# Value and gate groups of four attention blocks as pairs with two Strassen blocks each, and the attention tail moved into the next pair

## The reference, cut to what matters

```
proj = h @ w_in                      # (256 x 2048) @ (2048 x 14336), columns xr yr q k v g_rnn g_attn
q = partial_rope(q); k = partial_rope(k)
p = softmax(causal(q @ k.T * 128 ** -0.5))      # 16 heads of 128, 256 x 256 each
o = p @ v
attn_out = o @ w_attn_proj
merged = sigmoid(g_rnn) * rnn_out + sigmoid(g_attn) * attn_out
x = x + merged @ w_mix_out
```

## Time and profile before

| | us |
|---|---|
| median of 3 runs (1747.55 to 1747.8) | 1747.65 |
| the profiled execution | 1748.19 |
| its span in the trace | 1745.9 |
| PE busy | 1734.6 (99%) |
| VectorE busy | 1327.0 (76%) |
| ScalarE busy | 986.8 (57%) |
| granted TensorE clock | 0.999 |

### The profile page before, as it was taken

How to read it: one execution, slowest core, us unless ns; L and a number is a source line. 1 busy time by engine, 2 the same in 40 slices (tenths; PEclk the granted TensorE clock), 3 DMA queues, 4 the chain that set the end, 5 groups by cost and what they waited for, 6 DMA issues and landing times.

```text
span 1745.9 us, 20385 instructions
## 1 busy us (share of the span) xinstructions
PE 1734.6 (99%) x7905; PEld 1439.8 (82%) x7905; DVE 1327.0 (76%) x1457; ACT 986.8 (57%) x1228; POOL 28.8 (2%) x54
## 2 busy tenths in 40 slices
PE   9999999999999999999999999999999999999998
PEld 7888888888888888888888888888888888888886
DVE  7577687887575757678765579888888888888887
ACT  6767678554555555555465465555555545555554
POOL 1100000000000000000000000000000000000000
PEclk9999999999999999999999999999999999999999
DMA  9565655666565655556865455566566566566663
GB/s 339 174 203 163 212 184 163 201 211 195 158 215 168 217 169 185 174 166 217 271 186 188 140 174 184 191 196 195 196 197 219 187 211 198 183 193 196 214 194 119
DMA packets 176048, 338.23 MB, mean 194 GB/s; under 512 B 10704, under 2 KB 15312, under 8 KB 175696
## 3 DMA queue, kind: packets, MB, share of 16 engines
q1 hardware_dynamic: 173376, 327.98, 59.4%
q0 software_dynamic: 1296, 5.24, 1.0%
q10 hardware_dynamic: 1280, 3.71, 0.5%
HBM read 334.80 MB, written 2.10 MB: 193 GB/s over the span
## 4 chain that ended last, share of the span: by engine, by line
PE 98%; DVE 1%; ACT 0%; DMA 0%; issue 0%; ACTq 0%; POOLq 0%; POOL 0%; DVEq 0%
PE group L486 29%; PE group L488 28%; PE group L487 28%; PE side L486 3%; PE side L487 3%; PE side L488 3%; PE side L549 2%; PE side L683 0%; PE side L667 0%; DMA x_T_in<-in_x_T 0%; PE side L621 0%; PE side L620 0%; PE side L619 0%; DVE x_res L1603 0%; PE side L665 0%
## 5 line engine op out<-in xcount | busy, mean ns | idle before, releaser
L858 ACT ACTIVATE w_hi<-w_raw 128x1024 fp32r<-128x1024 f32 x612 | 618.9, 1024 | 489.7 <-PE group L488 475.7
L1253 DVE TENSOR_TENSOR w_lo<-w_raw,w_hi 128x1024 fp32r<-128x1024 f32 x612 | 707.9, 1179 | 236.7 <-ACT w_hi L858 231.1
L486 PE MATMUL group<-w_hi,x_hi 128*128 128x512 f32 x1460 | 573.3, 393 | 0.6 <-DVE w_lo L1321 0.6
L488 PE MATMUL group<-w_hi,x_lo 128*128 128x512 f32 x1460 | 568.8, 390 | 0.0
L487 PE MATMUL group<-w_lo,x_hi 128*128 128x512 f32 x1460 | 568.2, 389 | 0.0
L486 PEld LDWEIGHTS group<-w_hi,x_hi 128*128 128x128 f32 x1460 | 274.2, 188 | 58.6 <-DVE w_lo L1253 2.3
L488 PEld LDWEIGHTS group<-w_hi,x_lo 128*128 128x128 f32 x1460 | 274.0, 188 | 57.7
L487 PEld LDWEIGHTS group<-w_lo,x_hi 128*128 128x128 f32 x1460 | 274.3, 188 | 55.5
L858 ACT ACTIVATE w_hi<-w_sums 128x1024 fp32r<-128x1024 f32 x98 | 103.9, 1061 | 179.3 <-PE group L488 150.3
L1253 DVE TENSOR_TENSOR w_lo<-w_sums,w_hi 128x1024 fp32r<-128x1024 f32 x98 | 119.9, 1224 | 92.1 <-ACT w_hi L858 92.1
L486 PE MATMUL group<-w_hi,inner_hi 128*128 128x512 f32 x274 | 107.0, 391 | 0.2 <-DVE x_res L1603 0.2
(11 more groups left out here) (329 smaller groups left out, 1792.8 us busy)
## 6 DMA issues: line engine op xcount, KB each, us to landing
w_raw<-in_w_in SPq DMA_DIRECT2D x223, 512.0 KB, 4.2
w_raw<-in_w_ffn_gate SPq DMA_DIRECT2D x88, 512.0 KB, 3.9
w_raw<-in_w_ffn_up SPq DMA_DIRECT2D x88, 512.0 KB, 4.5
w_raw<-in_w_ffn_down SPq DMA_DIRECT2D x88, 512.0 KB, 5.0
w_raw<-in_w_rnn_proj SPq DMA_DIRECT2D x32, 512.0 KB, 4.9
w_raw<-in_w_attn_proj SPq DMA_DIRECT2D x32, 512.0 KB, 4.6
w_raw<-in_w_mix_out SPq DMA_DIRECT2D x32, 512.0 KB, 4.9
w_raw<-in_w_xkv SPq DMA_DIRECT2D x16, 512.0 KB, 3.8
```

Of the source, the lines that this page charges most:

```text
L486: nc.tensor.matmul(out, h, whi[:, s, k, :], start=start, stop=False)
L488: return nc.tensor.matmul(out, l, whi[:, s, k, :], start=False, stop=stop)
L858: nc.scalar.activation(whi[:, s, ks], src[:, ks], ACT.Copy).then_inc(hi_ready[s], 1)
L1253: V_.tensor_tensor(wlo[:, s, ks], src[:, ks], whi[:, s, ks].bitcast(F32), ALU.subtract).then_inc(w_ready[s], 1)
```

## The change

The groups v and g_attn of each attention block become one pair with the plan "O0 O1 O2 W3 O4 W5 O6 O7", so 20 chunks (steps 0 to 19) in place of 16, with A of the two Strassen blocks at steps 6 and 12. KEY_PLAN becomes the same plan. They share the input sums x_sums. v is folded in v_tok, the gate in its columns of sig_attn (`fold_of` now takes the half). In the new pair both transposes stand at step 2, the scores, the mask and the maxima at step 4, and the exponentials at steps 6 and 7. What followed them (division, transposes of the probabilities, product with v, v_hi and v_lo) moves, as `attention_end`, into the next pair: division at step 1, transposes at step 3, product with v at step 5, v_lo at step 6; ScalarE also scales v at step 0 and makes the gate's tanh at step 1 there. PE gets a wait for the mask ahead of chunk A, and the wait for v_lo ahead of the first chunk D of that next pair stays.

```diff
-KEY_PLAN = "O0 O1 W3 O2 O4 W5 O6 O7".split()
+KEY_PLAN = "O0 O1 O2 W3 O4 W5 O6 O7".split()
+VALUE_PLAN = "O0 O1 O2 W3 O4 W5 O6 O7".split()
...
# PE
+            def attention_end(c, j):
+
+                if c == 3:
+                    pe.wait_ge(sem("folded"), folds)
+                    pe.wait_ge(sem("prob"), j + 1)
...
+                    last.then_inc(sem("prob_T_ps"), 1)
+                if c == 5:
+                    pe.wait_ge(sem("prob_T"), j + 1)
+                    pe.wait_ge(sem("v_scaled"), j + 1)
...
+                        attention_end(c, j - 1)
                         if kind == "A" and kp == FIRST_SUM[first]:
-                            pe.wait_ge(sem("sums_lo"), 2)
                             pe.wait_ge(sem("folded"), folds)
                         if kind == "D" and kp == FIRST_SUM[first]:
                             pe.wait_ge(sem("attn_lo"), j)
                     folds += 1
-                for c in gemm_of("v", j, xhi, xlo):
+                first = ("v", j)
+                for c, kind, kp in pair_of(first, xhi, xlo, ks_hi, xs_lo, K_SUMS):
                     if c == 2:
                         pe.wait_ge(sem("k_rot"), j + 1)
+                        if folds > KG // 2:
+                            pe.wait_ge(sem("folded"), folds)
                         transpose(ktok, side[0], "k_T_ps")
-                    if c == 3:
                         pe.wait_ge(sem("q_rot"), j + 1)
                         transpose(qtok, side[1], "q_T_ps")
-                    if c == 5:
+                    if c == 4:
...
+                    if kind == "A" and kp == FIRST_SUM[first]:
+                        pe.wait_ge(sem("sums_lo"), 2)
+                        pe.wait_ge(sem("masked"), j + 1)
+                folds += 1
...
# ScalarE
+                first = ("v", j)
+                for c in splits(N0[first], len(STEPS[first])):
+                    first_fold(first, c)
...
-                for c in splits(N0["g_attn", j], CG):
-                    if c in (0, 1):
+                    if c in (6, 7):
                         act.wait_ge(sem("neg_max"), j + 1)
-                        for b in range(2 * c, 2 * c + 2):
+                        for b in range(2 * (c - 6), 2 * (c - 6) + 2):
...
# VectorE
+            def attention_end(c, j):
+
+                if c == 1:
+                    dve.wait_ge(sem("prob_exp"), j + 1)
+                    then(V_.reciprocal(rsum[:, :, :], psum_[:, :, :]))
...
+                if c == 6:
+                    dve.wait_ge(sem("attn_hi"), j + 1)
...
```

More of the change, by code:

```diff
@@ L103 @@
     elif _stage == "q" and _j > 0:
+        continue
+    elif _stage == "v":
+        PLACED.append(((_stage, _j), ("g_attn", _j), VALUE_PLAN))
+    elif _stage == "g_attn":
         continue
@@ L302, in slot_of, with fold_of @@
             return n % R, n // R
-        def fold_of(first):
-            return {"k": kq_fold, "attn_out": attn_fold}.get(first[0], fold)
+        def fold_of(first, half):
+            if first[0] == "v":
+                return sig_attn[:, :, first[1] * GW:(first[1] + 1) * GW] if half else vtok[:, :, :]
+            return {"k": kq_fold, "attn_out": attn_fold}.get(first[0], fold)[:, half]
         def raw_of(n):
@@ L381, in _ @@
                     pair(("k", j), (w_in,) * 2, 0, [IN_COLS[name] + j * GW for name in ("k", "q")])
-                in_group("v", j)
-                in_group("g_attn", j)
+                pair(("v", j), (w_in,) * 2, 0, [IN_COLS[name] + j * GW for name in ("v", "g_attn")])
             for q in range(0, KG, 2):
@@ L1066, in _ @@
                         first_fold(first, c)
-                        if c == 5 and j in (1, 2):
+                        attention_end(c, j - 1)
+                        if c == 12 and j in (1, 2):
                             mem_squares(2 * (j - 1))
@@ L1089, in _ @@
                                                             bias=nmax[:, tt, b:b + 1], accum_out=psum_[:, tt, b:b + 1])
-                        if c == 1:
+                        if c == 7:
                             last.then_inc(sem("prob_exp"), 1)
[L1092 to L1102, removed]
-                        evac_in("g_attn", j, [sig_attn[:, tt, j * GW:(j + 1) * GW] for tt in range(TT)], hrstd["x"], ACT.Tanh)
             def merge_hi(j):
@@ L1402, in fold_rest @@
             def fold_rest(first, c):
-                at_, fold = last_sum(first), fold_of(first)
+                at_, fold = last_sum(first), [fold_of(first, half) for half in range(2)]
                 if at_ is not None and c == at_ + 1:
@@ L1408, in fold_rest @@
                     wait_product(dve, N0[first] + c)
[L1409 to L1413 removed]
+                    then(V_.tensor_tensor(fold[1][:, 0, :], fold[0][:, 0, :], P6, ALU.subtract))
+                    then(V_.tensor_tensor(fold[0][:, 1, :], fold[1][:, 0, :], P7, ALU.subtract))
+                if at_ is not None and c == min(at_ + 2, len(STEPS[first]) - 2):
+                    V_.tensor_tensor(fold[1][:, 1, :], Q5, fold[0][:, 1, :], ALU.subtract)
+                    then(V_.tensor_tensor(fold[1][:, 0, :], Q5, fold[1][:, 0, :], ALU.subtract))
                     dve.sem_inc(sem("folded"), 1)
@@ L1418, in join @@
                 p, _ = buf_of(GI[first] + half)
-                fold = fold_of(first)
+                fold = fold_of(first, half)
                 wait_product(dve, end)
                 if last_sum(first) is None:
-                    V_.tensor_copy(fold[:, half], gps[p][:, :, :]).then_inc(taken[p], 1)
+                    V_.tensor_copy(fold, gps[p][:, :, :]).then_inc(taken[p], 1)
                 else:
-                    V_.tensor_tensor(fold[:, half], fold[:, half], gps[p][:, :, :], ALU.add).then_inc(taken[p], 1)
+                    V_.tensor_tensor(fold, fold, gps[p][:, :, :], ALU.add).then_inc(taken[p], 1)
             V_.memset(xTp[:, :, :], 0.0).then_inc(sem("pad_zero"), 1)
@@ L1553, in _ @@
                             join(first, half, END[("k", "q")[half], j])
-                for c in splits(N0["v", j], CG):
+                first = ("v", j)
+                count = len(STEPS[first])
+                for c in splits(N0[first], count):
+                    fold_rest(first, c)
                     if c == 0 and j > 0:
```

102 lines of the change are left out of this document (53 added, 49 removed).

## The result

| | median of its runs, us | runs (lowest to highest) | ratio to before [95%] |
|---|---|---|---|
| before | 1747.72 | 6 (1747.55 to 1747.97) | |
| changed | 1756.03 | 6 (1755.05 to 1756.41) | 1.0046 [1.0036, 1.0056] |

The account below looks back on a forecast made before the run. PE, busy 99% of the span, was taken to bound the kernel. New waits of 13.3 us less 5.4 us for 24 matmuls saved gave 7.9 us slower, 1755.5 us; 8-in-10 range 1750 to 1759.

Parts of the forecast that it names:

- 1: exponentials, 4 times, with the table load: Exponentials behind each block's first Strassen block make w_lo late: 1.85 us in each of 4 blocks, plus 1.4 once.
- 2: transposes of q, 4 times: Both transposes at step 2: PE waits for the rotation of q, 0.5 us a block with the restart.
- 3: v_lo ahead of D, 4 times: v_lo on VectorE behind w_lo of the next pair's first D comes late: 0.5 us a block.
- 4: division of the last block: In the first attn_out pair the division ends after PE wants it: 0.5 us once, with the restart.
- Place 1: Exponentials behind the first Strassen block: O4a 0.55 us late, second block's A 1.7 late; 1.85 a block with the restart.
- the restart: PE's cost of starting again after a wait: 0.17 us on top of each wait.
- (a): Rival: the gain lands and PE never waits, 1742.2 us; chance 0.07.
- (b): Rival: the exponentials cost nothing, the other waits leave 4.5 us against 5.4 saved, 1746.8 us; chance 0.07.
- (c): Rival: half the exponentials' cost, the sums being done before the late w_lo, 1752 us; chance 0.08.
- (d): Rival: waits drop PE's clock to 1.2 for a Strassen block each, 19 us more, 1775; 0.06 with other waits past 1759.
- (e): Rival: the change doesn't do what it says; given no chance.
- The table load: In block 0, between w_hi and the first exponential on ScalarE: 1.4 us once; by the skill's figure 1.3 us larger.

Follow-up runs that it names:

- experiment 1: The changed kernel with the two halves of the exponentials at steps 8 and 9 in place of 6 and 7: 1747.17 us, ratio to before 0.9997.
- experiment 4: The changed kernel with the transposes of q and ScalarE's copy of them back at step 3: 1753.84 us, ratio to before 1.0037.
- experiment 5: The changed kernel with v_lo at step 5 of the next pair in place of step 6: 1753.88 us, ratio to before 1.0034.
- experiment 7: The changed kernel with the last block's division one step earlier and the sums for attn_out one step later: 1755.45 us, ratio to before 1.0044.
- experiment 11: The changed kernel with the exponentials at steps 12 and 13, behind the second Strassen block: 1756.17 us, ratio to before 1.0049.

## Why the prediction was right

**The saving.** The pitch held. From one block's chunk A (its second matmul) to the next block's, the changed kernel needs 95.53 and 95.47 us (546.85, 642.38, 737.85), the kernel before 94.1 (573.56 to 667.66, from the key pair's first chunk A to the next one). That is 1.4 more, with 1.36 saved: 2.76 us of delay a block, where 1.85 + 0.5 + 0.5 = 2.85 was forecast. With all places mended a block takes 92.8 (540.90 to 633.66), 1.3 less than before.

**The terms,** each by the kernel that takes it away, in the medians and in the stretch of the traces, and by the rows of block 1 or of the place:

| term | forecast, us | taken away, medians, us | taken away, stretch of the traces, us | from rows, us |
|---|---|---|---|---|
| 1: exponentials, 4 times, with the table load | 8.8 | 8.86 (experiment 1) | 8.44 | 4 x 1.78 + 1.41 = 8.5 |
| 2: transposes of q, 4 times | 2.0 | 2.19 (experiment 4) | 1.69 | 4 x 0.42 = 1.7 |
| 3: v_lo ahead of D, 4 times | 2.0 | 2.15 (experiment 5) | 2.03 | 4 x 0.48 = 1.9 |
| 4: division of the last block | 0.5 | 0.58 (experiment 7) | 0.64 | 0.51 |
| sum | 13.3 | 13.8 | 12.8 | 12.6 |
| less 24 matmuls | 5.4 | 5.4 | 5.4 | 5.4 |
| slower by | 7.9 | 8.4 | 7.4 | 7.2 |

Measured 8.3 in the medians, 7.57 in the stretch. The stretch takes 414.11, 420.86, 420.52 and 421.91 us in experiments 1, 4, 5 and 7, against 422.55. With all four places mended at once it takes 409.77, 12.78 less, as much as the four taken away one by one: the waits do not hide one another. The rows agree with the stretch to 0.2 us. The medians are about 1 us higher in sum, which no wait in the stretch accounts for; behind the stretch, where all kernels are the same, the way to the last matmul's end takes from 900.9 to 902.0 us, from trace to trace. Term by term, then, the forecast was 0.3 to 0.4 us high in the first two places, right in the third and 0.1 low in the last; in the total these misses and the half microsecond outside nearly cancel, which is luck, but a small one.

**Place 1, step by step.** O4a's w_lo ended at 539.93 with the matmul due at 539.40: 0.53 late, forecast 0.55. That of A ended 11.84 us behind the first block's start, forecast 11.9; 1.64 late, forecast 1.7. The delay with the restart is 1.78, forecast 1.85 (1.7 + 0.17, as the prediction rounded it). So the walk through the two queues was off by 0.06 us.

**The rivals.** (a), the gain lands, and (b), only the small waits: out, with 8.9 us at place 1. (c), half of place 1: out as well; the chain of waits shows the sums run after the late w_lo, not before it. (d), the clock: the window of nearly all four blocks, with 15 of the 17 waits, still shows 1.00, and the mean of the execution is 0.999 as before (length, busy us of the engines, clock, DMA share, GB/s):

```profile
383.00:754.00 371.00, 363.43 (x1667) 299.11 (x1666) 290.51 (x342) 208.33 (x279) 4.38 (x8) 1.00 0.59 184
```

PE shows only 363.43 us busy of 371 there. Its longest pause in the blocks is this one, in block 0:

```profile
444.42 0.50 PE L492 MATMUL group<-w_hi,x_hi 128*128 128x512 f32 x1 [1.83 <-DVE w_lo L1282]
```

The clock stayed at 1.00, its 2.4 GHz level, behind it as behind the 16 others (the window 370 to 900 has all of them and shows 1.00 too). The Trainium skill ("TensorE: Matmul & The Clock Gate", HAM oscillation) warns that idle gaps of PE bring its clock down; no pause here did. (e), that the change doesn't do what it says: the 7881 matmuls and the rows above say it does.

**The table load** was right in place, and its size is the one term with two readings. In ScalarE's queue it costs 1.41 us between the copy and the first exponential, as in the earlier trace rows:

```profile
437.93 1.06 ACT L875 ACTIVATE w_hi<-w_sums 128x1024 fp32r<-128x1024 f32 x1 [1.66 <-PE group L494]
439.00 1.28 ACT L1127 ACT_TABLE_LOAD   x1
440.30 0.40 ACT L1127 ACTIVATE prob<-prob,nmax 128x128 f32<-128x128 f32 x1
```

Taken off the path it gave 1.4 us in the waits, 1.47 in the stretch of the traces (421.08 against 422.55) and 1.76 in the medians. The Trainium skill ("ScalarE: Activation LUTs", What ACT_TABLE_LOAD costs) gives 2.66 us for a switch; its 1283 ns for the load agree with the 1.28 us here, the drain that it adds does not appear in any of these rows.

**The expectation that was furthest off** is that of experiment 11, by 1.8 us. Over the kernel before it had 6.7 us, and the stretch of its trace takes 422.00 us, 7.0 more. It left out that the last block's division comes later (761.60 where 760.44 was due, 1.16 late in place of 0.51), and its 0.3 to 1.2 us for the wait at the join hold for the lateness in two blocks (1.06), while the other two waits are short. The rest of the 1.8 us lies outside the stretch, and no run says what it is. What the experiment settles is the rival that only the weight sums had cost so much (1751.5): it is out.

## What to carry to other kernels

Where engines prepare work some steps ahead in one queue, an inserted instruction costs what goes beyond the margin: the work of the bound engine that lies between the release of a slot and its next use. Here that was 3.4 us behind a Strassen block (between three ordinary chunks it is 8.2) and 6.8 us two steps later, for a refill of 2.6 us and 1.8 us of exponentials; the first lost 8.4 to 8.9 us in all, the second nothing. So the place of an addition is found by walking the queue from a release to the next due time and further to the next full stretch. Average load does not tell the orders apart (VectorE at 81% is harmless in one, at 78% PE loses 13 us in another). And a change that shortens the bound engine's steps takes from every such margin, so things that stood well before have to be walked again.

## What the runs showed of the hardware

- A wait of PE costs its lateness and about 0.15 us more up to the second matmul, whether the lateness is 0.53 us (0.68 of delay at O4a) or 0.88 us (545.60 due and 546.48 ready; 1.02 of delay at A); it was 0.17 at 0.33. The first matmul after it has a row of 0.50 us in place of 0.39, and the pitch stays a little over 0.227 us for some matmuls more: the next 8 took 1.86 us behind A's wait (0.233 each), the next 22 took 5.06 behind O4a's (0.230 each).
- The busy sum of PE hides a part of the waits: it is 1734.6 us before and 1734.7 with 24 matmuls (5.4 us) fewer, since the pitch is 0.227 and a row lasts 0.39. With the waits gone it is 1729.1. The waits of its weight loads show what it hides.
- 17 pauses of PE between 423 and 778 us, the longest 1.83 us, left the granted clock at 1.00.
